# Second expert layer with one-hot products in place of row gathers, row stores and a combining stage

## The reference

```python
scores = jax.nn.sigmoid((h @ w_router).astype(jnp.float32))
_, idx = lax.top_k(scores + e_bias.astype(jnp.float32), TOP_K)
wts = jnp.take_along_axis(scores, idx, axis=-1)
wts = wts / wts.sum(-1, keepdims=True) * ROUTE_SCALE
...
def expert_block(args):
    tok, e = args
    xb = h_pad[tok]
    a = jax.nn.silu(xb @ w_gate[e]) * (xb @ w_up[e])
    return a @ w_down[e]
...
shared = (jax.nn.silu(h @ s_gate) * (h @ s_up)) @ s_down
return routed + shared
```

## Time and profile before

| | us |
|---|---|
| median of 3 runs | 3181.65 |
| lowest, highest | 3179.26, 3190.05 |
| profiled execution, its own time | 3187.65 |
| profiled execution, its span | 3185.8 |
| mean granted clock of TensorE | 0.909 of 2.4 GHz |
| busy, PE / DVE / ACT / POOL | 2647.9 / 1182.5 / 844.7 / 244.1 |

### The profile page before, as it was taken

How to read it: one execution, slowest core, us unless ns; L and a number is a source line. 1 busy time by engine, 2 the same in 40 slices (tenths; PEclk the granted TensorE clock), 3 DMA queues, 4 the chain that set the end, 5 groups by cost and what they waited for, 6 DMA issues and landing times. The chain is left out here.

```text
span 3185.8 us, 44029 instructions
## 1 busy us (share of the span) xinstructions
PE 2647.9 (83%) x17438; PEld 1840.2 (58%) x17438; DVE 1182.5 (37%) x1846; ACT 844.7 (27%) x1250; POOL 244.1 (8%) x214
## 2 busy tenths in 40 slices
PE   5787599999997599598764557999889989989798
PEld 4666443344342486343222226988549989887698
DVE  2444632211112624411110026438645454445443
ACT  1141111111111223111100005426524344334442
POOL 0000200221003110100110020000100000000000
PEclk7898699999998799699887778999999999999899
DMA  8824699999987334699999975533325344341551
GB/s 326 318 91 180 273 392 426 398 364 411 423 362 318 147 99 179 245 385 422 407 425 415 425 294 225 198 110 134 132 93 225 145 186 196 119 167 55 198 198 73
DMA packets 124505, 810.85 MB, mean 255 GB/s; under 512 B 31784, under 2 KB 33448, under 8 KB 71976
## 3 DMA queue, kind: packets, MB, share of 16 engines
q1 hardware_dynamic: 90648, 718.88, 56.3%
q0 software_dynamic: 19168, 53.65, 4.4%
q10 hardware_dynamic: 14512, 35.89, 2.9%
HBM read 762.12 MB, written 56.84 MB: 257 GB/s over the span
## 5 line engine op out<-in xcount | busy, mean ns | idle before, releaser
L2391 PE MATMUL psum<-second_x_hi,ffn_up_hi 128*128 128x256 f32 x1408 | 402.2, 286 | 22.1 <-DVE ffn_up_lo L2500 22.1
L2391 PE MATMUL psum<-second_x_lo,ffn_up_hi 128*128 128x256 f32 x1408 | 401.6, 285 | 0.0
L2391 PE MATMUL psum<-second_x_hi,ffn_up_lo 128*128 128x256 f32 x1408 | 401.4, 285 | 0.0
L1585 PE MATMUL psum<-experts_ahead_ring_up,moe_cols 128*64 128x512 f32 x1568 | 360.6, 614 | 34.5 <-issue 34.4
L1949 DVE TENSOR_TENSOR experts_gated<-experts_silu,psum 128x256 f32<-128x256 f32 (+1 forms) x93 | 34.1, 366 | 693.5 <-ACT experts_silu L1735 693.5
L2391 PEld LDWEIGHTS psum<-second_x_hi,ffn_up_hi 128*128 128x128 f32 x1408 | 273.6, 194 | 25.0 <-DVE ffn_up_lo L2500 23.6
L1592 PE MATMUL psum<-experts_ahead_ring_up,moe_cols 128*32 128x256 f32 x2432 | 178.0, 444 | 117.1 <-issue 116.6
L2391 PEld LDWEIGHTS psum<-second_x_lo,ffn_up_hi 128*128 128x128 f32 x1408 | 273.6, 194 | 1.4
L2391 PEld LDWEIGHTS psum<-second_x_hi,ffn_up_lo 128*128 128x128 f32 x1408 | 273.5, 194 | 0.0
L1585 PEld LDWEIGHTS psum<-experts_ahead_ring_up,moe_cols 128*64 128x64 f32 x1568 | 115.1, 141 | 245.8 <-issue 245.0
L2468 DVE TENSOR_TENSOR ffn_up_lo<-second_ring_up,ffn_up_hi 128x4096 fp32r<-128x4096 f32 x40 | 177.0, 4426 | 110.3 <-ACT ffn_up_hi L2428 110.3
(11 more groups left out here) (518 smaller groups left out, 4413.9 us busy)
## 6 DMA issues: line engine op xcount, KB each, us to landing
experts_ahead_ring_up<-in_experts SPq DMA_DIRECT2D x130, 2048.0 KB
experts_ahead_ring_down<-in_experts SPq DMA_DIRECT2D x130, 1024.0 KB
second_ring_up<-in_ffn SPq DMA_DIRECT2D x44, 2048.0 KB, 9.2
second_ring_down<-in_ffn SPq DMA_DIRECT2D x44, 1024.0 KB
results<-experts_y ACTq DMA_DIRECT2D x49, 512.0 KB
second_ring_up<-in_attn_w_qkv SPq DMA_DIRECT2D x9, 2048.0 KB
results<-ab_zeros SPq DMA_DIRECT2D x32, 512.0 KB
ab_ahead_ab_in_w<-in_w_mod SPq DMA_DIRECT2D x6, 2048.0 KB
```

Source lines behind the costliest of these rows:

```text
L1585: last = nc.tensor.matmul(psum[64 * e:64 * e + 64, bank, :], x[:, k, 64 * e:64 * e + 64], w[:, k, :, :].rearrange("p a n -> p (a n)"), sta ...
L2391: last = nc.tensor.matmul(psum[:, 2 * m + kind, 0:LAT], w[:, j, k, at], h[:, k, :], start=k == 0 and which == 0, stop=k == KD - 1 and whic ...
```

## The change

`h_dram`, `results` and `who_dram` are no longer used by layer 1, `combine_norm_stage` no longer runs for it, and `token_rows_stage`, `transpose_stage` and `experts_stage` are replaced by two stages. Layer 0 is as before.

`resident_rows_stage` computes h on DVE alone, splits it into `h_hi` (fp32r, ACT) and `h_lo` (POOL), and PE turns h into columns; meanwhile SP issues the ten router tables and right behind them 9 expert loads (5 up, 4 down).

`resident_experts_stage` numbers each token's place in each of its experts. For each job DVE builds a one-hot matrix `hot` (128 tokens x 128 slots for each tile) by comparing slot numbers with places (`build`). Columns of the gathered tokens are products of `h_hi` and `h_lo` with `hot` (`turn`), in fp32r, for a group of jobs that together have 256 slots; half a group at a time. The transposed one-hot (`turn_hot`, copied on DVE to `hot_t`) times the job's result, split into `y_hi` (ACT) and `y_lo` (DVE), is added in four PSUM banks that stay open over all jobs (`combine`). A slot's weight (`shares_of_slots`) is folded into the product on DVE. That leaves one bank for up products (UP), one for transposes (TURN) and two for down products and columns (DOWN). The order of the jobs changes too: pairs 0 to 3 full, the thirds of pairs 2 and 3, pairs 4 to 15 full, 16 thirds. The groups of jobs are (0,1), (2,3), (4,5,6), (7,8) to (15,16) in pairs, (17,18,19), then fours, and the last two.

```diff
+class ResidentPlan:
...
+        first = [job for job in wide if job[1] < KEPT // 2]
+        routed = first + both + [("third", p, 64) for _, p, _ in both] + wide[len(first):] + slim
...
+        self.group_of = [u // 2 for u in self.unit_of]
...
+        self.groups = [[i for i, g in enumerate(self.group_of) if g == group] for group in range(self.group_of[-1] + 1)]
...
+def resident_rows_stage(nc, name, psum, ident, x, h, vectors, h_hi, h_lo, cols, loads):
...
+                nc.vector.scalar_tensor_tensor(h[:, t, :], vec[:, 0, :], 1.0, x[:, t, :], ALU.add, ALU.mult).then_inc(scaled, 1)
+                vectors.wait(dve, 1)
+                dve.wait_ge(scaled, t + 1)
...
+            for t in range(tok_tiles):
...
+                act.wait_ge(shifted, t + 1)
+                nc.scalar.activation(h_hi[:, t, :], h[:, t, :], ACT.Copy).then_inc(his, 1)
...
+                nc.scalar.activation(to, of, ACT.Copy)
...
+                nc.gpsimd.tensor_tensor(h_lo[:, t, :], h[:, t, :], h_hi[:, t, :], ALU.subtract).then_inc(los, 1)
...
+def resident_experts_stage(nc, name, psum, ident, ring, cols, inputs, h_hi, h_lo, acc, x, vector_rows):
...
+    turn_at = {}
+    for g, first in enumerate(group_first):
+        if g >= 1:
+            turn_at[first - 2], turn_at[first - 1] = (g, 0), (g, 1)
...
+        SUMS, UP, TURN, DOWN = 0, 4, 5, 6
...
+        def gather_parts(g):
...
+            span = slice(slot_of[group[0]], slot_of[group[-1]] + 1)
+            if kinds == {"full"} and len(group) == 2:
+                return [(0, 256, lambda t: hot[:, span, t, :])]
+            if kinds == {"third"}:
+                return [(0, 64 * len(group), lambda t: hot[:, span, t, :].rearrange("p j (e h s) -> p j e h s", e=2, h=2)[:, :, :, 0, :])]
+            return [(plan.column(i), P if routed[i][0] == "full" else 64, lambda t, i=i: gather_operands(i, t)) for i in group]
...
+                for t in range(tok_tiles):
+                    last = nc.tensor.matmul(psum[:, TURN, 0:2], hot_f32[:, slot, t, :], shares(t), start=t == 0, stop=t == tok_tiles - 1)
...
+                for t in range(tok_tiles):
+                    last = nc.tensor.transpose(psum[:, TURN, 256 + t * P:256 + (t + 1) * P], hot_f32[:, slot, t, :], ident[:])
...
+            def turn(g, half):
+                for k in range(4 * half, 4 * half + 4):
+                    bank = psum[:, DOWN + k % 4 // 2, k % 2 * 256:k % 2 * 256 + 256]
+                    for at, width, operand in gather_parts(g):
+                        terms = [(part, t) for t in range(tok_tiles) for part in (h_hi, h_lo)]
+                        for which, (part, t) in enumerate(terms):
+                            last = nc.tensor.matmul(bank[:, at:at + width], part[:, t, k * P:(k + 1) * P], operand(t), start=which == 0, stop=which == len(terms) - 1)
+                last.then_inc(turned, 1)
+
+            def combine(kind, place, at=0, closes=False):
+
+                for t in range(tok_tiles):
+                    for half in range(2):
+                        to = hot_t[:, place, half if kind != "full" else 0, t * P:(t + 1) * P]
+                        first = half * BANK if kind == "full" else at
+                        for part in (y_hi, y_lo):
...
+            for i in range(n_routed + 1):
+                j = n_shared + i
+                if i < n_routed:
+                    kind = routed[i][0]
+                    wait_up(j)
+                    pe.wait_ge(turned_out, 4 * (plan.group_of[i] + 1))
+                    up_product(kind, cols[(plan.group_of[i] + 1) % 2][:, :, plan.column(i):plan.column(i) + (P if kind == "full" else 64)], jobs[j][1]).then_inc(ups, 1)
+                pe.wait_ge(prepared_out, i + 1)
...
+                    pe.wait_ge(hot_ready, i + 2)
+                    pair = routed[i + 1][1]
+                    last = shares_of_slots(slot_of[i + 1], lambda t: share[:, t, 2 * pair:2 * pair + 2])
+                if 1 <= i <= n_routed:
...
+                    pe.wait_ge(rest_known, 1)
+                if i >= 2:
+                    pe.wait_ge(y_his, i - 1)
+                    pe.wait_ge(y_los, i - 1)
+                if i in turn_at:
+                    g, half = turn_at[i]
+                    pe.wait_ge(hot_ready, plan.groups[g][-1] + 1)
+                    pe.wait_ge(turned_out, 4 * g + 2 * half)
+                    turn(g, half)
+                if i >= 2:
+                    combine(routed[i - 2][0], i % 2).then_inc(combined, 1)
+                if 1 <= i <= n_routed:
+                    if i in turn_at:
+                        g, half = turn_at[i]
+                        pe.wait_ge(turned_out, 4 * g + 2 * half + 2)
+                    down_of(j - 1)
+                if i == owners_at:
+                    pe.wait_ge(owners_ready, 1)
+                    nc.tensor.matmul(psum[:, DOWN + 1, 0:n], every, greater, start=True, stop=True).then_inc(owners, 1)
...
+            pe.wait_ge(y_his, n_routed)
...
+            combine("third", 1, closes=True).then_inc(combined, 1)
...
+            def copy_turned(g, half):
+                act.wait_ge(turned, 2 * g + half + 1)
+                width = 64 * sum(2 if routed[i][0] == "full" else 1 for i in plan.groups[g])
+                for b in range(2):
+                    k = 4 * half + 2 * b
+                    nc.scalar.activation(cols[(g + 1) % 2][:, k:k + 2, 0:width], psum[:, DOWN + b, :].rearrange("p (k n) -> p k n", k=2)[:, :, 0:width], ACT.Copy).then_inc(turned_out, 1)
...
+            for i in range(n_routed + 1):
+                if i < n_routed:
+                    silu_of(n_shared + i)
+                if i in turn_at:
+                    copy_turned(*turn_at[i])
...
+                    act.wait_ge(downs, n_shared + i)
+                    if i >= 2:
+
+                        act.wait_ge(combined, i - 1)
+                    if routed[i - 1][0] == "full":
+                        nc.scalar.activation(y_hi[:].rearrange("p (h n) -> p h n", h=2), psum[:, DOWN:DOWN + 2, :], ACT.Copy).then_inc(y_his, 1)
+                    else:
...
+
+                dve.wait_ge(prepared, i + 2)
+                if i + 1 < n_routed:
+                    v.tensor_copy(slot_share[0:64, (i + 1) % 2:(i + 1) % 2 + 1], psum[0:64, TURN, 0:1])
+                    last = v.tensor_copy(slot_share[64:128, (i + 1) % 2:(i + 1) % 2 + 1], psum[64:128, TURN, 1:2])
+                if i >= 1:
+                    if i >= 3:
+                        dve.wait_ge(combined, i - 2)
+                    last = turned_hot(routed[i - 1][0], (i - 1) % 2)
+                last.then_inc(prepared_out, 1)
...
+                if i >= 1:
+                    dve.wait_ge(y_his, i)
+                    if routed[i - 1][0] == "full":
+                        v.tensor_tensor(y_lo[:].rearrange("p (h n) -> p h n", h=2), psum[:, DOWN:DOWN + 2, :], y_hi[:].rearrange("p (h n) -> p h n", h=2), ALU.subtract).then_inc(y_los, 1)
+                    else:
...
+            general(dve, body)
+            dve.wait_ge(combined, n_routed)
...
+            def residual(t):
+                halves = acc[:, t, :].rearrange("p (h n) -> p h n", h=2)
+                then(v.tensor_tensor(halves, psum[:, SUMS + 2 * t:SUMS + 2 * t + 2, :], vec[:, 2, :].rearrange("p (h n) -> p h n", h=2), ALU.mult))
...
+    def second_experts():
+
+        with Stage(nc, "moe1") as st:
+            cols = [a[:, 2:4, :].rearrange("p t d -> p (t d)").rearrange("p (k n) -> p k n", n=LAT) for a in (acc, x)]
+            inputs = ResidentInputs(nc, st, i["w_router"][1], i["moe_bias"][1], i)
+            ring = ExpertRing(nc, st, i["experts"], N_EXPERTS + 1, RESIDENT)
+            h_hi, h_lo = (st.sbuf(k, [P, 2, D], F32R) for k in ("h_hi", "h_lo"))
+
+            def columns_loads(sp):
+                inputs.loads(sp)
+                for kind, item in (("up", 0), ("down", 0), ("up", 1), ("up", 2), ("down", 1), ("down", 2), ("up", 3), ("up", 4), ("down", 3)):
+                    place = ring.first + (N_EXPERTS if item == 0 else RESIDENT.items[item])
+                    (ring.load_up if kind == "up" else ring.load_down)(sp, item, place)
+
+            resident_rows_stage(nc, "h2_1", psum, ident, x, acc, scale_shift1, h_hi, h_lo, cols[0], columns_loads)
+            resident_experts_stage(nc, "experts1", psum, ident, ring, cols, inputs, h_hi, h_lo, acc, x, [i["ln2_g"][1], i["ln2_b"][1], gate(1, 5, 0)])
 
```

627 lines of the change are left out of this document (601 added, 26 removed).

## The result

The kernel with the change took 3137.5 us (median of four, 3134.3 to 3141.4), the kernel before 3183.4 beside it: ratio 0.985, 95% interval 0.983 to 0.988, 46 us. The forecast was 3125, its range 3090 to 3165. The sign and the range hold. The parts of the sum hold less well, and the experiments are about them.

The account below looks back on a forecast made before the run. Weight transfers bound most of the layer, PE one window, gathers and waits the combining. A gain of 57 us, 26 in the stage and 31 behind it, gave 3130.6 on the profiled basis, 3125 for the median; range 3090 to 3165.

Parts of the forecast that it names:

- The head: Start of the layer: weight loads from 1301.8, 10.7 us earlier; by_rank near 1338; routed work near 1355.
- A full job: Each full job on PE: 15.1 us against 14.8 of weight transfers, so bound by PE, narrowly.
- The mixed halves: Gather products of groups (4,5,6) and (17,18,19): 48 at 0.115, 5.5 us, 3.6 more in each of four halves.
- PE's part: Job iterations 0 to 16, where PE sets the pace: 254 us together, from 1355 to 1609.
- The transfers' part: Third jobs from 1609, where the full queue sets the pace: 217 us of loads to 1841, last down at 1846.
- rival 3: Third jobs at half clock: 18 us each on PE, 3.2 over their weights, 51 in all; 3176, chance 0.05.
- The tail: From the last down product to the layer's last pass: 20 us with waits, against 51.7 before.
- The stage's gain: Experts' stage up to the last down product: 26 of the 57 us gain, the other 31 behind it.
- Rival 1: Weight queue never starves, full jobs at or below 14.8: gain 115 us, 3066; chance 0.10.
- 2 (full jobs 2 us longer): 2 us left uncovered in each of 17 job iterations: +34 us, 3159; chance 0.17.
- 4 (fp32r at the price of fp32): combine and turn at fp32 price: +10.5 us on each of 17 iterations, 3338; chance 0.08 with stalls its size.
- rival 5: Stage not shortened, only the tail's 31 us won: 3150, inside the range; chance 0.60 together with the forecast.

Follow-up runs that it names:

- uniform order: Kernel with the change, two slim third jobs moved behind the thirds of pairs 2 and 3, so all groups are of one kind: 3109.4 us, ratio 0.979.
- thirds early: Kernel with the change, groups of one kind and four slim third jobs ahead of full pairs 2 and 3: 3101.7 us, ratio 0.975.
- the ranks first: On top of the order with four slim thirds early, PE's steps for the experts' order moved ahead of the shared expert's second up product: 3100.2 us, ratio 0.975.

## Why the prediction was right, and where it was not

**The head** was right within 4 us: on the clock of before the loads started at 1301.7 (forecast 1301.8), the experts' stage at 1308.1 (1309), `by_rank` at 1334.2 (1338), routed work at 1350.9 (1355). The 425 GB/s of the forecast was an estimate that no row of before shows; the queue did run at it among the thirds and, in the uniform order, beside the full jobs.

**A full job** was put at 15.1 and took 15.54. `turn` and `combine` were 0.1 too low each. The step that failed is 11.7 - 1.1 = 10.6 for what is left of the old job: up, down and gate transposes take 7.02 + 3.59 + 0.36 = 10.97. The trace of before has both reasons:

```profile
1448.10 1.09 PE L1573 MATMUL psum<-all_ident,experts_x_rows 128*128 128x128 f32 x8
1449.03 0.38 PE L1598 MATMUL psum<-all_ident,experts_gated 128*128 128x128 f32 x2
```

From start to start the eight row transposes take 0.93 and not the 1.09 of their busy time, which runs into the next row. And there up, down and gate transposes had 6.92 + 3.54 + 0.31 = 10.77, 0.2 less than now; why they take longer now is open. No cross-engine step came into view, as forecast.

**The mixed halves** were put at 0.115 for each product, from the earlier trace rows; the trace has 0.111 for 64 and for 128 columns. The Trainium skill's figure in TensorE: Matmul & The Clock Gate, section Back-to-back issue gap, about 81 ns at 128 columns, does not hold for these fp32r products: 0.111 is what the measurement shows. The same page of the Trainium skill, section LDWEIGHTS (loading the stationary operand), puts a load of 128 columns of weights at their number divided by 1.2, 107 ns; with that the trace agrees better. What the sum lacked is the falls of the clock.

**PE's part** took 267.1 us (1340.95 to 1608.09), forecast 254. By iterations: 9.8, 14.9, 22.2, 20.6, 10.1, 10.3, 13.8, eight of 15.54, 19.0, 22.2, against 9.8, 15, 18.7, 18.7, 10, 10, 13.6, eight of 15.1, 18.7, 18.7. Of the 13.1 more, 8.1 are falls of the clock in the mixed halves, 3.5 the full jobs, 1.5 the rest. Less the 4 of the head it leaves PE's part 9 us late.

**The transfers' part** was put at 237 us from 1609 to the end of the last down product, and took 243 (1608.57 to 1851.70). The queue kept 425 GB/s, as forecast; its thirds came 14.8 apart. The 6 us are at the end, for which I had allowed 5: PE had been idle for 4.9, ran the last up product in 6.2 us instead of the 3.7 at full clock, and needed 10 more to the end of the last down product, with two `combine`, a down product and 1.5 of waiting for the gates' copy ahead of it. The last down product ended at 1861.7 on the clock of before, forecast 1846. That the third jobs cost PE half of their clock is rival 3's mechanism; its condition, that 18 us of PE would then be on the path, did not come: most of a third is back at full clock once PE has work.

**The tail** was put at 20 and took 22.1, of 51.7.

**The stage's gain** is where the argument was weakest. 69 us of transfers were not used between 1291.7 and 1616.7. The sum contained that (it made PE's part longer than its transfers), but the prediction read the idle queue as a price of full jobs at 15.1 against 14.8, "narrowly" bound by PE. The runs show that the full jobs, in a row and with a full ring behind them, cost nothing: with the same 15.5 on PE, uniform groups have the queue at 425 GB/s beside them. What costs is that PE starts behind a full ring and meets the mixed groups and the slot-holding pairs 2 and 3 there. Rival 1 had this as its objection and was rightly not the forecast.

**The rivals.** 1 (never starves) did not come, though half of the way to it was open by the order alone. 2 (full jobs 2 us longer): no. 4 (fp32r at the price of fp32): no, 0.12 and 0.23. 5 (only the tail) was nearer than I had it: 30 of 39.5 are the tail. The forecast's number was 12 us low because of a stage that gave 10 instead of 26. That it was not 17 low, as the layer was (39.5 against 57), is luck: the medians differ by 46, 6 us more than the layer gives, in parts of the program that no line of the change touches. And the range held rival 5 as well, so that it alone does not confirm the sum.

One row shown ahead of the prediction is miscopied: in the order of the kernel before, the row of L1545 has 128x64 and not 64x64. Nothing rests on it.

**A faster version**: the order with thirds early beats both kernels, 3101.7, ratio 0.975 (0.974 to 0.977), with one line changed; the version with the ranks first is the same within the interval.

## What to carry to other kernels

When a ring of weights feeds an engine that works through jobs of unlike shape, the order of the jobs can be worth as much as a saving in the jobs (here 40 us of 3137, up to 22 of them by keeping unlike jobs out of one group): put those that need little of the engine where it is behind, and look at the bytes moved, not at the share, to see what the queue lost. Take a step's price from the distance between starts and not from its busy time, above all when it is subtracted. And a gain behind a stage (here 30 us of combining) is safer to count than one inside it, which the next limit may take.

## What was new of the hardware

- fp32r products of 64 and of 128 columns, each with its own 128 x 128 weights, came 0.111 us apart, those of 256 columns 0.12, of 512 0.23. Widening from 64 to 128 cost nothing.
- Among products of 64 columns (with some of 128) the granted clock fell from 2.4 to 1.2 GHz while PE was busy without a gap, for 3.4 to 10.2 us at a time, in 19 of 20 halves that had 32 products of 64 and 16 of 128 columns. With half of the products left out (four halves), or with all 48 made 128 wide (two halves, and two with each product twice), it stayed at full. How long a fall lasts differs between executions: 8.1, 9.7 and 16.1 us lost in all in three traces.
- A DMA share of 1.00 stood for 408 GB/s when loads were issued just as slots came free, at PE's pace (405), and for 425 when the queue had work waiting. The earlier trace rows has 415 at such a share, which the prediction put down to stores and gathers; this stage has neither, so that was not all of it. What makes the difference is open.
